# Value projections made as features with all 272 tokens moving, and turned into token rows by TensorE

## The reference, cut to what matters

```python
def fox_mixer(h, w_in, b_f, q_gain, k_gain, w_out):        # layers 0 and 3
    proj = h @ w_in
    q, k, v, gate, f = jnp.split(proj, [D_MODEL, 2 * D_MODEL, 3 * D_MODEL, 4 * D_MODEL], axis=-1)
    q = rmsnorm(q.reshape(B, L, H, Dh), q_gain) * (Dh ** -0.5)
    k = rmsnorm(k.reshape(B, L, H, Dh), k_gain)
    log_f = jax.nn.log_sigmoid((f + b_f).astype(jnp.float32))
    c = jnp.cumsum(log_f, axis=1).transpose(0, 2, 1)
    ...                                                      # p = softmax(q k + c_q - c_k), o = p v
    o = o * jax.nn.sigmoid(gate)
    return (o @ w_out).astype(h.dtype)

def gla_mixer(h, w_in, w_alpha2, b_alpha, o_gain, w_out):  # layer 1
    proj = h @ w_in
    q, k, v, r, a_lr = jnp.split(proj, [GLA_QK, 2 * GLA_QK, 2 * GLA_QK + GLA_V, 2 * GLA_QK + 2 * GLA_V], axis=-1)
    g = jax.nn.log_sigmoid((a_lr @ w_alpha2 + b_alpha).astype(jnp.float32)) / GLA_GATE_NORMALIZER
    ...                                                      # o = chunked linear attention with decays cumsum(g)
    o = rmsnorm(o, o_gain) * jax.nn.silu(r.reshape(B, L, H, GLA_DV))
    return (o.reshape(B, L, GLA_V) @ w_out).astype(h.dtype)
```

## Time and profile before

| what | value |
|---|---|
| median of 3 runs | 2933.85 us (2931.7 to 2938.04) |
| profiled execution, its time | 2932.17 us |
| its span | 2930.3 us |
| PE, share of the span | 92% |
| VectorE | 69% |
| ScalarE | 52% |
| mean granted clock of PE | 0.959 |
| items of the first attention | 1270 to 1394 us |
| of the gated-linear mixer | 1684 to 1804 us |
| of the second attention | 2548 to 2666 us |

### The profile page before, as it was taken

The page is one execution under the profiler, slowest core; times in us unless marked ns, Lnnn a source line. Parts: engine busy times, 40 slices in busy tenths (PEclk is TensorE's granted clock), DMA queues, the critical chain, the costliest instruction groups (busy, mean ns, idle before and its releaser), DMA issues. The chain is left out here.

```text
span 2930.3 us, 55882 instructions
## 1 busy us (share of the span) xinstructions
PE 2704.2 (92%) x21488; PEld 2451.5 (84%) x21488; DVE 2011.1 (69%) x3504; ACT 1520.8 (52%) x2586; POOL 108.1 (4%) x142
## 2 busy tenths in 40 slices
PE   7998989997797999889899998999988899998999
PEld 5855579995766999779699988999888799997999
DVE  2157479994465999676667774677765577786677
ACT  3257368884554888554543454434742343446443
POOL 1010011100000111000000000000000000000000
PEclk9999989997897999979999999999989999999999
DMA  8281179999224999934045533455530155442453
GB/s 294 87 297 64 63 255 372 369 366 327 87 73 140 358 359 355 356 94 134 30 161 177 170 113 101 164 178 161 178 115 1 44 173 172 159 144 73 159 186 115
DMA packets 286160, 528.96 MB, mean 181 GB/s; under 512 B 14288, under 2 KB 207104, under 8 KB 285328
## 3 DMA queue, kind: packets, MB, share of 16 engines
q1 hardware_dynamic: 273312, 499.72, 49.2%
q0 software_dynamic: 9216, 12.61, 1.4%
q10 hardware_dynamic: 3440, 13.98, 1.2%
HBM read 526.16 MB, written 21.06 MB: 187 GB/s over the span
## 5 line engine op out<-in xcount | busy, mean ns | idle before, releaser
L2113 DVE TENSOR_TENSOR W_lo<-ring,W_hi 128x1024 fp32r<-128x1024 f32 x384 | 452.7, 1221 | 46.1 <-ACT W_hi L2027 44.6
L2300 PE MATMUL ps<-H_part,W_hi 128*128 128x272 f32 (+2 forms) x1800 | 415.1, 305 | 25.5 <-DVE H_part L2204 12.7
L2833 ACT ACTIVATE W_hi<-ring 128x1024 fp32r<-128x1024 f32 x264 | 263.1, 1049 | 294.0 <-PE ps L2806 185.4
L2784 PE MATMUL ps<-room_part,W_hi 128*128 128x272 f32 (+1 forms) x1408 | 404.4, 287 | 5.0 <-DVE room_part L2204 5.0
L2027 ACT ACTIVATE W_hi<-ring 128x1024 fp32r<-128x1024 f32 x384 | 384.5, 1052 | 39.1 <-PE ps L1941 17.2
L2785 PE MATMUL ps<-room_part,W_hi 128*128 128x272 f32 (+1 forms) x1408 | 403.6, 287 | 0.0
L2786 PE MATMUL ps<-room_part,W_lo 128*128 128x272 f32 (+1 forms) x1408 | 402.8, 286 | 0.0
L2300 PEld LDWEIGHTS ps<-H_part,W_hi 128*128 128x128 f32 x1800 | 301.8, 191 | 43.7 <-issue 28.7
L2873 DVE TENSOR_TENSOR W_lo<-ring,W_hi 128x1024 fp32r<-128x1024 f32 x264 | 314.1, 1219 | 10.3 <-ACT W_hi L2833 9.4
L2300 PE MATMUL ps<-H_part,W_lo 128*128 128x272 f32 (+2 forms) x1024 | 303.9, 297 | 0.0
L1939 PE MATMUL ps<-W_hi,A_split_hi 128*128 128x256 f32 x1024 | 294.1, 287 | 4.5 <-DVE A_split_lo L2119 4.5
(11 more groups left out here) (517 smaller groups left out, 5864.2 us busy)
## 6 DMA issues: line engine op xcount, KB each, us to landing
ring<-in_w_down SPq DMA_DIRECT2D x108, 1024.0 KB, 4.8
ring<-in_w_gate_up SPq DMA_DIRECT2D x88, 1024.0 KB, 5.0
ring<-in_w_gate SPq DMA_DIRECT2D x64, 1024.0 KB, 7.4
ring<-in_w_up SPq DMA_DIRECT2D x64, 1024.0 KB, 7.4
ring<-in_w_mod SPq DMA_DIRECT2D x48, 1024.0 KB, 5.4
ring<-in_fox_w_in SPq DMA_DIRECT2D x32, 1024.0 KB, 5.9
ring<-in_gdn_w_in SPq DMA_DIRECT2D x16, 1024.0 KB, 5.9
ring<-in_gla_w_in SPq DMA_DIRECT2D x12, 1024.0 KB, 5.2
```

What stands on the lines that cost most here:

```text
L2113: dve.tensor_tensor(lo, c.ring[:, (self.g0 + p) % SLOTS, W], hi.bitcast(F32), ALU.subtract)\
L2300: mm = pe.matmul(self.out(i), a, b, start=(k == 0 and n_part == 0), stop=(k == KC - 1 and n_part == 2))
L2784: pe.matmul(out, wh[:, k, M], hi, start=(k == 0), stop=False)
L2833: act.activation(self.slot_parts(p)[0][:, C], c.ring[:, g % SLOTS, C], ACT.Copy).then_inc(c.hi_done, 1)
```

## The change

- The values become feature items of all 272 tokens, two per slot, 8 in place of 12 (`turned_features` for `normed_tokens`). ScalarE moves them, unscaled, into one of four buffers: `m["OT"][:, 1:5, :]`.
- At every second step behind, PE turns a pair of such tiles into token rows (`turn_values`: 3 tiles of tokens by 2 transposes), into the parts of the two banks that the pair has left, and ScalarE moves these, times `rs_rows`, to where the values were (`value_rows`: 3 instructions). A bank is free for PE when these are out (`vacated`); a buffer is free for ScalarE when PE has turned it (`buffer_free`).
- An attention now has 32 items (values 16 to 23), the gated-linear mixer 24 (values 8 to 15). What stands beside them is moved to other steps: in the attention the logits 21 to 20 (PE) and 22 to 21 (ScalarE), their turning 23 to 22, bias 24 to 23, exp and log 25 to 24, "log" 26 to 25, cumsum 28 to 26, its copy 30 to 28. The heads keep their steps. In the mixer `SCORES` has one level per step; what follows comes 2 to 4 steps earlier by number; the sums of squares, which stood one step behind the last outputs, stand in their step; the first silu comes ahead of the copies of the turned keys.

```diff
@@ Stream.product
         if i >= 4:
-            pe.wait_ge(*self.moved(i - 4))
+            pe.wait_ge(*self.vacated(i - 4))
@@ NormProject
+    def vacated(self, i):
+        if not self.is_value(i):
+            return self.moved(i)
+        odd = (i - self.values[0]) % 2
+        return (self.scalar_done, self.act.at("values", i - odd, 2 * odd))
+    def buffer_free(self, act, i):
+        if self.is_value(i) and i >= self.values[0] + 4:
+            odd = (i - self.values[0]) % 2
+            act.wait_ge(self.tensor_done, self.pe.at("values", i - 4 - odd))
+    def turn_values(self, pe, i):
+        first, _, buffers = self.values
+        for j in (i, i + 1):
+            pe.wait_ge(*self.moved(j))
+        for t, (t0, tn) in enumerate(TILES2):
+            for j in (i, i + 1):
+                tr = pe.transpose(self.value_bank(i, t)[0:tn, (j - i) * P:(j - i + 1) * P], buffers[:, (j - first) % 4, t0:t0 + tn],
+                                  self.c.s("ident"))
+        tr.then_inc(self.tensor_done, self.pe.mark("values", i))
+    def value_rows(self, act, i):
+        first, rows, _ = self.values
+        act.wait_ge(self.tensor_done, self.pe.at("values", i))
+        for t in (2, 1, 0):
+            tn = TILES2[t][1]
+            act.activation(rows[0:tn, t, (i - first) * P:(i - first + 2) * P], self.value_bank(i, t)[0:tn], ACT.Copy,
+                           scale=self.c.rs_rows[0:tn, t:t + 1]).then_inc(self.scalar_done, self.act.mark("values", i, t))
@@ NormProject.tensor and .scalar, after the item and ahead of the work beside it
+            if self.turns_values(i):
+                self.turn_values(pe, i - 2)
...
+            if self.turns_values(i):
+                self.value_rows(act, i - 2)
@@ FoxProject.beside_tensor
-        if i == 28:
+        if i == 26:
             pe.wait_ge(self.vector_done, self.dve.at("log", 2))
@@ FoxProject.beside_scalar
-        if i == 25:
+        if i == 24:
             for t, (t0, tn) in enumerate(TILES2):
                 w = m["w"][0:tn, t, :]
                 act.wait_ge(self.vector_done, self.dve.at("abs", t))
@@ FoxProject.beside_vector
-        if i == 26:
+        if i == 25:
             for t, (t0, tn) in enumerate(TILES2):
                 dve.wait_ge(self.scalar_done, self.act.at("log", t))
@@ GlaProject
-    SCORES = {9: -1, 11: 0, 12: 1, 14: 2, 15: 3, 16: 4, 17: 5, 19: 6}
-    GATED = {23: (0, 1), 24: (2, 3), 25: (4,), 26: (5,), 27: (6, 7)}
+    SCORES = {9: -1, 10: 0, 11: 1, 12: 2, 13: 3, 14: 4, 15: 5, 16: 6}
+    GATED = {20: (0, 1), 21: (2, 3), 22: (4, 5), 23: (6, 7)}
@@ GlaProject.beside_tensor
-        if i == 20:
-            pe.wait_ge(*self.moved(19))
+        if i == 17:
+            pe.wait_ge(self.scalar_done, self.act.at("values", 14, 0))
-        if 22 <= i < 26:
+        if 19 <= i < 23:
             pe.wait_ge(self.vector_done, self.dve.at("state", 1))
-        if i == 26:
-            pe.wait_ge(*self.moved(24))
+        if i == 22:
+            pe.wait_ge(*self.moved(20))
@@ turned_features, in place of normed_tokens
     for j, s in enumerate(slots):
+        for m in range(2):
+            move = (lambda x: lambda act, ps: act.activation(x, ps, ACT.Copy))(dst[:, (2 * j + m) % 4, :])
+            out.append((s, "feature", m * P, P, 0, T2, Move("scalar", move)))
```

More of the change, by code:

```diff
@@ L2391, with __init__ @@
 class NormProject(Stream, Normed):
-    def __init__(self, core, gain, sources, items, sq, behind=None, zero=()):
+    def __init__(self, core, gain, sources, items, sq, behind=None, zero=(), values=None):
         Stage.__init__(self, core)
+        self.values = values
         self.stream(core, sources, items)
@@ L2453, in vector, with is_value, turns_values, value_bank @@
             self.beside_vector(dve, i)
+    def is_value(self, i):
+        return self.values is not None and self.values[0] <= i < self.values[0] + KC
+    def turns_values(self, i):
+        return self.is_value(i - 2) and (i - self.values[0]) % 2 == 0
+    def value_bank(self, i, t):
+        return self.c.ps[:, (i + (t == 2)) % 4, 256 * (t == 0):256 * (t == 0) + 2 * P]
+    def vacated(self, i):
+        if not self.is_value(i):
+            return self.moved(i)
+        odd = (i - self.values[0]) % 2
+        return (self.scalar_done, self.act.at("values", i - odd, 2 * odd))
+    def buffer_free(self, act, i):
+        if self.is_value(i) and i >= self.values[0] + 4:
[17 more added lines that the diff above has]
+                           scale=self.c.rs_rows[0:tn, t:t + 1]).then_inc(self.scalar_done, self.act.mark("values", i, t))
     def beside_tensor(self, pe, i):
@@ L2483, in __init__ @@
     def __init__(self, core, gain, sources, items, sq, behind, zero, m, heads, wf, bf):
-        super().__init__(core, gain, sources, items, sq, behind, zero)
+        super().__init__(core, gain, sources, items, sq, behind, zero, (16, m["V"], m["OT"][:, 1:5, :]))
         self.m, self.heads, self.wf, self.bf = m, heads, wf, bf
@@ L3139 @@
     LOW_RANK, SUMS = 6, 0
-    SCORES = {9: -1, 11: 0, 12: 1, 14: 2, 15: 3, 16: 4, 17: 5, 19: 6}
-    GATED = {23: (0, 1), 24: (2, 3), 25: (4,), 26: (5,), 27: (6, 7)}
+    SCORES = {9: -1, 10: 0, 11: 1, 12: 2, 13: 3, 14: 4, 15: 5, 16: 6}
+    GATED = {20: (0, 1), 21: (2, 3), 22: (4, 5), 23: (6, 7)}
     def __init__(self, core, gain, sources, items, sq, behind, zero, m, squares):
-        super().__init__(core, gain, sources, items, sq, behind, zero)
+        super().__init__(core, gain, sources, items, sq, behind, zero, (8, m["V"], m["values"]))
         self.m, self.squares = m, squares
@@ L3293, in beside_scalar @@
                .then_inc(self.scalar_done, self.act.mark("scores"))
-        if i >= 20:
+        if i >= 16:
             act.wait_ge(*self.moved(i))
-            x = m["R"][:, i - 20, :]
-            act.activation(x, x, ACT.Silu).then_inc(self.scalar_done, self.act.mark("silu", i - 20))
-        if i == 19:
+            x = m["R"][:, i - 16, :]
+            act.activation(x, x, ACT.Silu).then_inc(self.scalar_done, self.act.mark("silu", i - 16))
+        if i == 16:
             for t in range(2):
@@ L3303, in beside_scalar @@
                    .then_inc(self.scalar_done, self.act.mark("turned", t))
-        if 22 <= i < 26:
-            for u in (2 * (i - 22), 2 * (i - 22) + 1):
+        if 19 <= i < 23:
+            for u in (2 * (i - 19), 2 * (i - 19) + 1):
                 act.wait_ge(self.tensor_done, self.pe.at("o", u))
@@ L3398, in beside_vector @@
         for u in self.GATED.get(i, ()):
-            if i == 27 and u == 6:
+            if i == 23 and u == 6:
                 dve.wait_ge(self.scalar_done, self.act.at("head root"))
@@ L3982, in normed_features, with turned_features @@
     return out
-def normed_tokens(c, dst, slots):
+def turned_features(dst, slots):
     out = []
     for j, s in enumerate(slots):
[L3988 to L3991, removed]
+        for m in range(2):
+            move = (lambda x: lambda act, ps: act.activation(x, ps, ACT.Copy))(dst[:, (2 * j + m) % 4, :])
+            out.append((s, "feature", m * P, P, 0, T2, Move("scalar", move)))
     return out
@@ L4064, in gla @@
     m["masks"] = acc[:, at + 1536:at + 1728].rearrange("p (l t) -> p l t", l=6)
+    m["values"] = m["OT"][:, 1:5, :]
     m["E"], m["lr"], m["one"], m["hr"] = [m["e"], m["g"]], m["OT"][:, 0, :], m["OT"][:, 4:8, :], m["b"][:, 0, :]
@@ L4069, in gla @@
                          normed_features(c, m["Q"], [0, 1], 0, T2, scale=P ** -0.5) + normed_features(c, m["K"], [2, 3], 0, T2)
-                         + normed_tokens(c, m["V"], range(4, 8))
+                         + turned_features(m["values"], range(4, 8))
                          + normed_features(c, m["R"], range(8, 12), 0, T2), squares, behind, [m["A0"], m["D"], m["A"]], m, squares)
```

34 lines of the change are left out of this document (18 added, 16 removed).

## The result

The changed kernel takes 2951.03 us (median of 5, 2946.61 to 2953.62), against 2933.85 (median of 5): ratio 1.0055, 95% interval 1.004 to 1.007. It is slower by 17.2 us, and the prediction said 16.2. Its profiled execution has a span of 2949.4 us, 19.1 more than before.

The account below looks back on a forecast made before the run. The prediction took TensorE (PE) to bound the kernel, busy 92% of the span. Its terms, 3.7 + 4.0 + 4.1 + 5.0 = 16.8 us longer, put the median at 2950.7, said as 2950 us; range 2934 to 2958.

Parts of the forecast that it names:

- the running sum of the first attention: First attention: the cumsum starts at 80.6 instead of 70.9, 9.7 us late; with fewer items behind it, stage 3.7 longer.
- PE's wait: Both attentions, after item 26: PE waits 9.6 us for VectorE's "log" before the cumsum.
- The wait for the value rows at item 26: First attention: item 26 needs the bank that value rows (22) leave at 68.0, and ends at 71.0.
- the prediction's signs: First attention: PE idle 8 to 11 us before cumsum, five table loads, not three; mixer: two waits of about 4 us.
- the second case of rival (e): Attention chain: a table switch takes twice 1.3 us, 1.3 more for each of four: 2961 us; 2% chance.
- The first case of rival (e): VectorE behind earlier, clock 0.5 after each wait: attentions 7 to 8 us longer each, mixer 8: 2959 to 2965; (e) 7%.
- Rival (b): Item 26 of both attentions: the wait for "log" costs PE little; 2926.8 us; 8% for a result under 2928.
- rival (d): All three stages: PE alone decides everywhere, 7.3 us gained per stage, 22 us less in all, 2912 us; 2% chance.
- The clock: PE at a lower clock after the new waits: 2 us for each attention, 1 for the mixer, 5.0 in all.
- The mixer: Gated-linear mixer: score-level chain starts the K-V product at 71.0, not 64.6; stage 4.1 us longer, plus 1 for the clock.
- the wait at the sums of squares: Mixer's end: sums of squares follow the last outputs at once, waiting for ScalarE's copy and square, 0.9 us.
- 3.7 + 2, 4.0 + 2, 4.1 + 1: Us longer, first attention, second attention, mixer: the stage's own loss plus its share for the lower clock.

Follow-up runs that it names:

- e3_cumsum_late: The changed kernel, with PE's running sum at step 30 instead of 26 and ScalarE's copy of it at 31 instead of 28: 2931.39 us, ratio 0.9988.
- e4_log_first: The changed kernel, with VectorE's "log" at the end of step 24, ahead of the last weight slot and head 15: 2936.47 us, ratio 1.0006.
- mended order: The order of `e5_attention_order`: "log" at VectorE's step 24, and ScalarE's value rows, root, exp and log ahead of item 24's sigmoid; 2921.35 us.
- e2_mixer_only: The changed kernel with both attentions put back as before, so only the mixer is changed: 2936.26 us, ratio 1.0003.
- e5_attention_order: `e4_log_first`, plus ScalarE doing the value rows and the work beside item 24 ahead of its sigmoid: 2921.35 us, ratio 0.9964.

## Why the prediction was right

**Point by point, the attentions.** Against the stage's start, the running sum of the first attention came 10.2 us later than before (110.45 against 100.28); predicted 9.7. PE's wait was predicted as 9.6 and was 9.62 and 9.66; the other 0.5 is that PE reached it later, since item 26 began 0.2 later than worked out and took 3.28 us to the wait and not 3.0.

The wait for the value rows at item 26: the prediction gave its end, 68.0, and not its length; from item 23's end at 59.4, two items and a set of transposes put PE there at 66.1 to 66.4, so 1.6 to 1.9, and 1.61 and 1.84 were measured. ScalarE loaded five tables between head 14's root and item 25's sigmoid, as the prediction's signs said. The table switches cost 1.3 us each, with the next instruction 0.02 us behind a load (1370.70 + 1.28, then 1372.00), so the second case of rival (e) falls. The drain that the Trainium skill ("ScalarE: Activation LUTs", What ACT_TABLE_LOAD costs) adds to a load is not in this trace.

`e3_cumsum_late` and `e4_log_first` show the cause, not only the place: with only the wait moved or cut, 19.6 and 14.6 us came back, of a loss of 17.2. The first case of rival (e) gave 7 to 8 us for each attention, which is nearer to the 6.7 and 7.4 measured than the forecast's 5.7 and 6.0, but 8 for the mixer, where 2.0 came; its parts add up to 22 or 24 us, so to 2956 to 2958 and not to 2959 to 2965. Rival (b), that the wait costs PE little, is refuted by its 9.6 us, and rival (d) was right on what PE alone would give: 7.4 measured in the mended order, 7.3 predicted.

**The clock.** Predicted 2 us for each attention. Measured, as the stage's loss, less the delay of the running sum, plus what the two missing items give back: 6.7 - 10.2 + 6.0 = 2.6 (unrounded) in the first, 7.4 - 10.1 + 5.7 = 3.0 in the second. The half clock lasted 6.0 us behind the wait and not 4.6. A small miss, to the same side in both. `e4_log_first` adds that it isn't the length of the wait that sets it: behind 2.38 us the price was as high.

**The mixer.** This is the term that was mis-sized: predicted 4.1 + 1, measured 2.0 in the stage. The chain up to the K-V product was right. The first wait is 3.77 (predicted 4.0). Level 1 starts 53.0 us into the stage, as predicted (37.0, where the stage began at -16.0 on that clock), though its wait is 2.65 and not 4.3: the clock fell on level 0 and the item ahead of level 1, in this window of the changed kernel:

```profile
1738.00:1741.40 3.40, 3.40 (x82) 3.36 (x83) 3.40 (x3) 0.88 (x1) 0.00 (x0) 0.52 0.02 5
```

so 1.7 us that would have been wait were slow work. The K-V product starts 86.96 us into the stage in place of 80.62, 6.3 later, predicted 6.4. What was wrong stands behind that product. Before, the product's second half took 3.63 us at the lower clock; after, it took 1.99:

```profile
1781.87 1.99 PE L3278 MATMUL ps<-room,ACC 128*128 128x256 f32 x8
...
1810.09 1.49 PE L3300 MATMUL ps<-room,small 128*32 128x272 f32 x16
```

I had carried the half clock of before over into the time that stays equal. In the changed kernel it fell 4 us earlier, on the item ahead, where it took the place of a wait (granted 0.52 from 1775.5 to 1779.0). That is 1.6 us. The second is the wait at the sums of squares, 0.9 in the sum: the 16 matmuls took 1.49 with what they waited, before 1.14, so 0.35. The 1 us for the clock in the rest was not needed in this profile. That it was not is in part luck. The old mixer's stage was 122.1 us in all four profiles that have it. The mixer as changed took 124.1 in two profiles (the changed kernel, `e2_mixer_only`) and 125.5 to 125.6 in three (`e3_cumsum_late`, `e4_log_first`, `e5_attention_order`), with the same instructions; in `e3_cumsum_late` and `e4_log_first` the granted clock fell once more, 70 us into the stage, and in `e5_attention_order` it fell on the K-V product. So the new mixer costs 2.0 to 3.6 us, by where the lower clock falls, and less than the 5.1 of the sum in every profile; what decides where it falls is not shown.

**Sum.** Predicted 16.8 us in the stages, 3.7 + 2, 4.0 + 2, 4.1 + 1; measured 16.2: 6.7, 7.4, 2.0. The attentions were 2.4 too low together and the mixer 3.1 too high, so a part of the agreement in the total is two misses that cancel. That is luck; the mechanism and the length of its wait were forecast.

## What to carry to other kernels

When an item list written by hand gets shorter, what stands beside it must be asked not "how many items ahead" but "behind what in its own engine's list": the running sum went from two steps behind "log" (28 and 26) to one (26 and 25), and waited 9.6 us, since "log" stood behind a slot and a head, and these behind a sigmoid and a slot of ScalarE. Two steps would not have been enough: an item later is 3.0 us later, so by estimate 6.6 us of wait would be left; no run has the running sum there. Put the short chain that PE waits for ahead of the long instructions of the same step, and group by table: here two edits of the order alone gave 30 us (2951.0 to 2921.4). And a saving on the bounding engine can be real and unseen at once; a run that only takes the wait away, like `e3_cumsum_late`, shows it.

## What the runs showed that I had not expected

- A wait's price in clock does not follow its length. After 9.62 us PE was granted 0.50 for 6.0 us of work, after 8.89 us for 4.6, which is 3.0 and 2.3 us more. After 2.38 us, with 1.84 us one item earlier, it was 6.4 us of work (`e4_log_first`); after 1.84, 1.52 and 1.66 us with two or more items between them it stayed at 1.00 (`e3_cumsum_late`).
- A table load runs ahead of the wait of its activation: at 1364.78 it was done 3.12 us before VectorE's result came. So a load costs nothing where its engine waits anyway, and the same load costs 1.3 us where the chain runs through it.
- Where the lower clock falls can decide 1.6 us of a stage: the K-V product's second half, the same eight products, took 3.63 us before, 1.99 in the changed kernel and 2.95 in the mended order.
